# A two-block transformer kernel: squares, first norm, bias tables, memory rows and a token-major feed-forward, all changed at once

## The chip, the cores and the metric

The kernel runs on one core of a Trainium2 chip. The metric is the device time of one execution in microseconds (us). Three executions of the kernel before took 2737.11, 2744.5 and 2745.8 us; the median is 2744.5 us.

## The reference, cut to what matters

Everything is float32, the sequence has 256 tokens and the model 2048 features. The first block has two layers, the second one:

```
first block, for l in 0, 1:
    h = rms_norm(x, norm_g[l]);  z = h @ w_in[l]             # 2048 -> 16 heads, 4 x 128 columns each
    6 dilated heads (rotary), 6 neighbourhood heads (bias from na_rpb, + mask), 4 memory heads
    (the memory heads' keys and values: rms_norm(mem) @ w_mem_kv[l])
    x = x + (attention * silu(gate)) @ w_out[l]
second block:
    h = rms_norm(x);  z = h @ w_in;  state space mixer, differential attention with
    bias = rel_table[t5_bucket(k - q)], gates, x = x + m @ w_out
    h = rms_norm(x, norm2_w)
    x = x + (silu(h @ w_gate) * (h @ w_up)) @ w_down         # 2048 -> 5632 -> 2048
```

## The kernel before, in words

Activations are kept feature-major: `res`, `x_hi`, `x_lo` are [128 features, 16 blocks, 256 tokens]. A float32 product is made of three products of rounded parts: `w_hi*x_hi + w_hi*x_lo + w_lo*x_hi` (L1692 to L1694). Weights come in chunks of 512 KB, [128, 8*128], into a ring of four (`w_raw`, `RING`). SyncE loads chunk n+4 once `w_lo` of chunk n is made (L378), ScalarE rounds it to `w_hi` when TensorE has freed the slot (`split_hi`, L585), VectorE subtracts to `w_lo` (`split_lo`, L1077). A job is two chunks: 16 weight tiles, 48 matmuls of 256 token columns, for 128 output features. Four jobs are a period, one head takes one period, and there are 98 periods. Each engine's order is written out by hand; `prev` parts of a period work for the head before.

The names that matter for the change:

- Start. GpSimd squares `res` block by block and adds it up (L408, L403). TensorE sums the result over partitions with a matrix of ones (L1744, L1735) behind job 0 of the first period; VectorE makes `rstd` from it (`rstd_of`, L1098). The first weight chunk is split at block 3 of `x`.
- Neighbourhood bias. GpSimd stores the padded table of all 12 heads 64 times in `na_pad_d` in one transfer (L416), then for each of six heads loads four skewed pieces (L432), adds the mask (L436) and stores the bias (L438); then the second layer's six heads later.
- Memory. In heads 2 to 9 of layer 0 ScalarE rounds and squares two blocks of `mem` a head (`mem_blocks`, L621, L624); GpSimd adds the squares (L445), behind its six bias heads.
- Bias table of the second block. In the out projection of layer 0, behind jobs 4 to 11, TensorE makes one head's row of 511 values on all 128 partitions (L1767), VectorE copies it (L1287) and ScalarE's queue stores it in `rel_d` (L748). The same jobs make the state space tables: VectorE makes turns, ScalarE four activations (L601 to L606) and a store of 256 KB to `tab_d` (L608), whose landing it waits for before the next (`table`).
- Feed-forward. 11 groups of 4 feature blocks. In each: 4 gate jobs, 4 up jobs, 4 down jobs (`down`, L1978 to L1980), interleaved by `GATE_JOBS` and `UP_JOBS`. Gate and up are evacuated per 128 features (L1315), the sigmoid is ScalarE's (L946).

## Time and profile before

| | |
|---|---|
| median of three executions | 2744.5 us |
| the profiled execution | 2746.96 us |
| its span, first to last instruction | 2745.4 us |
| TensorE matmul busy | 2543.1 us, 93% |
| VectorE / ScalarE / GpSimd busy | 68% / 42% / 17% |
| first stretch, to 205.8 us: TensorE busy | 142.25 us |
| feed-forward, from about 1989 us to the end: TensorE busy | 749.15 of 756 us |

All times are microseconds from the span's start unless marked ns. PE is TensorE's matmul side, PEld its weight loads, DVE VectorE, ACT ScalarE, POOL GpSimd, SP SyncE; a q behind an engine's name is its sequencer or its transfer issues. "x" counts instructions. L12 is line 12. A transfer's landing time runs from issue to its last semaphore.

### The profile page before, as it was taken

Reading aid. Unit: us, or ns where it says so; the run is one execution under the profiler, and the core shown is the slowest. Engines: PE = TensorE matmul, PEld = TensorE weight load, DVE = VectorE, ACT = ScalarE, POOL = GpSimd, SP = SyncE. Lnnn points to the kernel's source line nnn. Section 1 sums busy time; section 2 is a strip of 40 time slices with the busy share of each in tenths; the row PEclk is TensorE's granted clock in tenths of the full one; section 3 lists DMA queues with packets and bytes.
Section 4 is the critical chain, followed back from the end, with each engine's and each line's share of the span. In section 5 each row is a group of like instructions: output and inputs, shape, how many; then the busy total and the mean of one; then the engine's idle time right before and its main releaser. Section 6 shows DMA issues by size and latency. Waiting matters only on the chain.

```text
span 2745.4 us, 54167 instructions
## 1 busy us (share of the span) xinstructions
PE 2543.1 (93%) x19776; PEld 2453.6 (89%) x19776; DVE 1877.5 (68%) x2716; ACT 1154.7 (42%) x1691; POOL 465.5 (17%) x501
## 2 busy tenths in 40 slices
PE   5779999989999999788888989699999999999999
PEld 5779999879999998778877777699999999999998
DVE  5667666778766667777778999665566555666654
ACT  3245444564444446544443222334433333333332
POOL 4310000123000002121136777310100000000000
PEclk8889999999999999999998999899999999999999
DMA  6655555567555555454444555465565555555554
GB/s 160 187 161 188 184 177 173 162 202 221 177 179 177 173 168 169 155 180 131 131 155 139 155 158 157 137 211 181 175 192 183 181 182 182 183 180 180 182 183 153
DMA packets 143166, 473.92 MB, mean 173 GB/s; under 512 B 18917, under 2 KB 25745, under 8 KB 142833
## 3 DMA queue, kind: packets, MB, share of 16 engines
q1 hardware_dynamic: 114048, 415.29, 47.1%
q0 software_dynamic: 9936, 28.44, 4.3%
q10 hardware_dynamic: 19104, 29.15, 3.2%
q8 instruction: 50, 0.82, 0.1%
q14 instruction: 28, 0.22, 0.0%
HBM read 447.01 MB, written 25.80 MB: 172 GB/s over the span
## 4 chain that ended last, share of the span: by engine, by line
PE 64%; DVE 14%; issue 10%; DMA 6%; ACT 3%; POOL 3%; DVEq 0%; ACTq 0%; POOLq 0%
PE z_ps L1692 17%; PE z_ps L1693 17%; PE z_ps L1694 17%; DVE w_lo L1077 5%; DMA tab_d<-arena 4%; DMA na_pad_d<-arena 1%; PE o_ps L1731 1%; PE s_ps L1713 1%; PE s_ps L1978 1%; PE s_ps L1979 1%; PE s_ps L1980 1%; PE o_ps L1980 1%; PE o_ps L1979 1%; PE o_ps L1978 1%; PE p_ps L1980 1%
## 5 line engine op out<-in xcount | busy, mean ns | idle before, releaser
L1077 DVE TENSOR_TENSOR w_lo<-w_raw,w_hi 128x1024 fp32r<-128x1024 f32 x782 | 985.3, 1291 | 434.5 <-ACT w_hi L585 422.8
L1692 PE MATMUL z_ps<-x_hi,w_hi 128*128 128x256 f32 x4224 | 1232.6, 292 | 49.9 <-DVE w_lo L1077 25.1
L1693 PE MATMUL z_ps<-x_lo,w_hi 128*128 128x256 f32 x4224 | 1212.5, 287 | 0.0
L1694 PE MATMUL z_ps<-x_hi,w_lo 128*128 128x256 f32 x4224 | 1210.9, 287 | 0.0
L585 ACT ACTIVATE w_hi<-w_raw 128x1024 fp32r<-128x1024 f32 x782 | 799.5, 1051 | 479.5 <-PE z_ps L1694 297.7
L1692 PEld LDWEIGHTS z_ps<-x_hi,w_hi 128*128 128x128 f32 x4224 | 829.1, 196 | 78.5 <-issue 64.2
L1693 PEld LDWEIGHTS z_ps<-x_lo,w_hi 128*128 128x128 f32 x4224 | 829.6, 196 | 1.4
L1694 PEld LDWEIGHTS z_ps<-x_hi,w_lo 128*128 128x128 f32 x4224 | 828.2, 196 | 0.0
L1692 PE MATMUL z_ps<-y_hi,w_hi 128*128 128x256 f32 x768 | 223.2, 291 | 25.3 <-DVE w_lo L1077 12.9
L1693 PE MATMUL z_ps<-y_lo,w_hi 128*128 128x256 f32 x768 | 220.6, 287 | 0.0
L1694 PE MATMUL z_ps<-y_hi,w_lo 128*128 128x256 f32 x768 | 220.3, 287 | 0.0
L1692 PEld LDWEIGHTS z_ps<-y_hi,w_hi 128*128 128x128 f32 x768 | 150.6, 196 | 35.3 <-issue 18.9
L1692 PE MATMUL z_ps<-m_hi,w_hi 128*128 128x256 f32 x576 | 167.7, 291 | 6.3 <-DVE m_lo L1512 3.6
L1694 PE MATMUL z_ps<-m_hi,w_lo 128*128 128x256 f32 x576 | 164.3, 285 | 0.0
L1693 PE MATMUL z_ps<-m_lo,w_hi 128*128 128x256 f32 x576 | 164.3, 285 | 0.0
L1693 PEld LDWEIGHTS z_ps<-y_lo,w_hi 128*128 128x128 f32 x768 | 150.8, 196 | 0.0
L1694 PEld LDWEIGHTS z_ps<-y_hi,w_lo 128*128 128x128 f32 x768 | 150.7, 196 | 0.0
L402 POOL TENSOR_TENSOR arena<-arena 128x256 f32<-128x256 f32 x32 | 26.5, 829 | 685.9 <-ACT arena L594 685.9
L1692 PEld LDWEIGHTS z_ps<-m_hi,w_hi 128*128 128x128 f32 x576 | 111.9, 194 | 7.8 <-DVE m_lo L1512 4.5
L1315 DVE TENSOR_TENSOR arena<-z_ps,rstd 128x256 f32<-128x256 f32 x120 | 50.7, 423 | 97.2 <-PE z_ps L1694 97.0
L1693 PEld LDWEIGHTS z_ps<-m_lo,w_hi 128*128 128x128 f32 x576 | 112.1, 195 | 0.4
L1694 PEld LDWEIGHTS z_ps<-m_hi,w_lo 128*128 128x128 f32 x576 | 111.8, 194 | 0.0
(314 smaller groups left out, 3202.4 us busy)
## 6 DMA issues: line engine op xcount, KB each, us to landing
w_raw<-in_w SPq DMA_DIRECT2D x784, 512.0 KB, 3.7
tab_d<-arena ACTq DMA_DIRECT2D x32, 256.0 KB, 5.0
res<-tab_d POOLq DMA_DIRECT2D x32, 256.0 KB, 2.9
sg_d<-arena ACTq DMA_DIRECT2D x32, 128.0 KB, 3.2
arena<-sg_d POOLq DMA_DIRECT2D x16, 256.0 KB, 3.9
arena<-in_dil_bias ACTq DMA_DIRECT2D x12, 256.0 KB, 2.8
arena<-na_pad_d POOLq DMA_DIRECT2D x48, 64.0 KB, 3.3
na_bias_d<-arena POOLq DMA_DIRECT2D x12, 256.0 KB, 2.9
```

Source lines behind the costliest of these rows:

```text
L402: pool.tensor_tensor(sq_sum[:, 1, :], sq_sum[:, 1, :], sqf[:], ALU.add)
L585: act.activation(w_hi[:, n % RING, :], w_raw[:, n % RING, :], ACT.Copy).then_inc(w_hi_ready, 1)
L1077: dve.tensor_tensor(w_lo[:, n % RING, :], w_raw[:, n % RING, :], w_hi[:, n % RING, :].bitcast(F32), ALU.subtract).then_inc(w_lo_ready, 1)
L1315: dve.tensor_tensor(dst, z_ps[c % ring][:, 0, :], rstd[:], ALU.mult).then_inc(z_free, 1)
L1692: pe.matmul(z, wh, hi[:, kt, :], start=(first and i == 0), stop=False)
L1693: pe.matmul(z, wh, lo[:, kt, :], start=False, stop=False)
L1694: m = pe.matmul(z, wl, hi[:, kt, :], start=False, stop=(last and i == len(kts) - 1))
L1713: m = pe.matmul(s_ps[:, t, :], q_t[:, t * P:(t + 1) * P], k_t[:], start=True, stop=True)
L1731: m = pe.matmul(o_ps[:, 0, :], v_tok[:, k, :], probs_t[:, k, :], start=(k == 0), stop=(k == NQ - 1))
L1978: pe.matmul(z, wh, y_hi[:, kt, :], start=(kt == 0), stop=False)
L1979: pe.matmul(z, wh, y_lo[:, kt, :], start=False, stop=False)
L1980: m = pe.matmul(z, wl, y_hi[:, kt, :], start=False, stop=(kt == F_GROUP - 1))
```

## The change

1. Squares of `x`: ScalarE squares four blocks in one activation of 128x1024 (4 of them); GpSimd adds them in 7 additions of 128x512. The first weight chunk is asked for behind the first quarter of `x` and is split at block 0.
2. The sums over partitions come behind job 1 instead of job 0 in both layers, and VectorE makes `rstd` behind the third pair of splits.
3. The padded neighbourhood table is stored once (`na_one_d`), and copied 64 times per head, DRAM to DRAM, in front of that head's four loads; GpSimd's loops over heads are unrolled.
4. The second block's bias table: one matmul for all 8 heads (8 partitions x 511), one copy, and 8 stores of ScalarE's queue that read one partition 64 times each, four behind job 7 and four behind job 11 of the out projection.
5. Memory blocks in heads 4 to 11; the state space constants one head later.
6. Feed-forward gate and up: tokens become the output's partitions. `x_hi`/`x_lo` tiles are the weights, four feature blocks of `w` the 512 moving columns. The result is scaled by `rstd` per partition (made on [128, 2] columns), the product [2, 128 tokens, 512] is turned back with 8 transposes a group. All 8 gate chunks, then 8 up chunks, then 8 down chunks. The down product is as before. The chunks are gathered from the same weight stream in runs of 256 floats, four per partition.

```diff
-            for n in range(KT):
-                pool.wait_ge(x_landed[n // 4], 16)
-                pool.wait_ge(sq_summed, summed(-1, n))
-                pool.tensor_tensor(sq[:], res[:, n, :], res[:, n, :], ALU.mult).then_inc(sq_ready, 1)
-                sum_squares(-1, n, False)
+            for i in range(4):
+                pool.wait_ge(sq_ready, 4 * i + 4)
...
+                    pool.tensor_tensor(sq_sum[:], sq_sum[:], lower, ALU.add).then_inc(xsq_step, 1)
...
-            pool.dma_start(na_pad_d.rearrange("c (h x) -> h c x", h=DEPTH * N_NA),
-                           rpb_pad.rearrange("h r x -> h (r x)").unsqueeze(1).to_broadcast(
-                               [DEPTH * N_NA, GRID_W, DR * DC])).then_inc(pad_stored, 16)
+            pool.dma_start(na_one_d, rpb_pad.rearrange("h r x -> h (r x)")).then_inc(pad_filled, 16)
...
+                    pool.dma_start(na_pad_d[lh:lh + 1].rearrange("h (c x) -> h c x", c=GRID_W),
+                                   na_one_d[lh:lh + 1].unsqueeze(1).to_broadcast([1, GRID_W, DR * DC])).then_inc(pad_stored, 16)
...
+                if n % 4 == 3:
...
+                    act.activation(x_sq[n // 4 % 2], res[:, n - 3:n + 1, :], ACT.Square).then_inc(sq_ready, 4)
...
-                with act.Fori(2, N_DIL) as h:
-                    head_period(p0 + h, l, h, ap["dil_bias"], mem=h - 2 if l == 0 else None)
+                with act.Fori(4 if l == 0 else 2, N_DIL) as h:
+                    head_period(p0 + h, l, h, ap["dil_bias"], mem=h - 4 if l == 0 else None)
...
-                        act.dma_start(rel_d[h].rearrange("(p x) -> p x", p=P),
-                                      rel_rows[:, h % 2, 0:REL]).then_inc(rel_stored[h % 2], 16)
+                        act.dma_start(rel_d[h:h + 1].rearrange("h (c x) -> h c x", c=CHUNK_ATT),
+                                      rel_rows[h:h + 1].unsqueeze(1).to_broadcast(
+                                          [1, CHUNK_ATT, REL])).then_inc(rel_stored, 16)
...
+            def ffn_gate(g):
+
+                dve.wait_ge(fg_s, g + 1)
+                for t in range(NQ):
+                    e = dve.scalar_tensor_tensor(out=act_t[:, t, :], in0=z_ps[t][:].rearrange("p a b -> p (a b)"),
+                                                 scalar=rstd_c[:, t:t + 1], in1=act_t[:, t, :],
+                                                 op0=ALU.mult, op1=ALU.mult)
...
+            def ffn_chunk(g, k, banks, wait_kt=False):
...
+                        pe.matmul(z[t], x_hi[:, kt, r], hi_w[:, :, i * P:(i + 1) * P], start=(kt == 0), stop=False)
+                        pe.matmul(z[t], x_lo[:, kt, r], hi_w[:, :, i * P:(i + 1) * P], start=False, stop=False)
+                pe.wait_ge(w_lo_ready, at + 1)
...
+                        m = pe.matmul(z[t], x_hi[:, kt, t * P:(t + 1) * P], lo_w[:, :, i * P:(i + 1) * P], start=False,
+                                      stop=(kt == KT - 1))
...
+            def turn_act(g, banks):
+
+                pe.wait_ge(fu_used, g + 1)
+                for h in range(2):
+                    for b in range(2):
+                        for t in range(NQ):
+                            m = pe.transpose(banks[h][:, b, t * P:(t + 1) * P],
+                                             act_t[:, t, (2 * h + b) * P:(2 * h + b + 1) * P], ident[:])
...
+            def blocks(base, j, step, n):
+
+                return bass.AP(ap["w"].tensor, (base + j // 4) * (P * CH * P) + (j % 4) * 2 * P,
+                               [[CH * P, P], [step * P * CH * P, n], [1, 2 * P]])
```

On TensorE in the first period, before (`p_ps<-arena,ones` are the sums over partitions; 48 matmuls are one job):

```order
L1694 MATMUL z_ps<-x_hi,w_lo 128x256
L1744 MATMUL p_ps<-arena,ones 128x256
L1735 MATMUL p_ps<-arena,ones 128x256
L1692 MATMUL z_ps<-x_hi,w_hi 128x256
L1693 MATMUL z_ps<-x_lo,w_hi 128x256
```

The pair is TensorE's instructions 49 and 50 there, behind 48 matmuls; in the changed kernel it is 97 and 98, behind 96, with the same neighbours.

On ScalarE in the out projection of layer 0, before, one job (`w_hi` is the split, the four activations in `arena` and `tab_d` the table, the next three the output block):

```order
L585 ACTIVATE w_hi<-w_raw 128x1024 x2
L601 ACTIVATE arena<-arena 128x256
L602 ACTIVATE arena<-arena 128x256
L604 ACTIVATE arena<-arena 128x256
L606 ACTIVATE arena<-arena 128x256
L608 DMA tab_d<-arena 128x512
L590 ACTIVATE x_hi<-res,gains 128x256
L593 ACTIVATE arena<-res,final_g 128x256
L594 ACTIVATE arena<-res 128x256
L748 DMA rel_d<-arena 128x511
```

And after, behind job 7 (and again behind job 11):

```order
L662 ACTIVATE x_hi<-res,gains 128x256
L665 ACTIVATE arena<-res,final_g 128x256
L666 ACTIVATE arena<-res 128x256
L826 DMA rel_d<-arena 64x1x511 x4
L657 ACTIVATE w_hi<-w_raw 128x1024 x2
L673 ACTIVATE arena<-arena 128x256
L674 ACTIVATE arena<-arena 128x256
L676 ACTIVATE arena<-arena 128x256
L678 ACTIVATE arena<-arena 128x256
L680 DMA tab_d<-arena 128x512
```

The eight single stores between jobs have become two runs of four, each ahead of the next table store on the same queue.

On TensorE in the feed-forward, before, three matmuls for one weight tile:

```order
L1692 MATMUL z_ps<-x_hi,w_hi 128x256
L1693 MATMUL z_ps<-x_lo,w_hi 128x256
L1694 MATMUL z_ps<-x_hi,w_lo 128x256
```

After, a part of a gate chunk of 12 (the next four of L2099 and L2100 repeat these), and the transposes:

```order
L2099 MATMUL z_ps<-w_hi,x_hi 128x512
L2100 MATMUL z_ps<-w_hi,x_lo 128x512
L2099 MATMUL z_ps<-w_hi,x_hi 128x512
L2100 MATMUL z_ps<-w_hi,x_lo 128x512
L2105 MATMUL z_ps<-w_lo,x_hi 128x512 x4
...
L2115 MATMUL p_ps<-ident,arena 128x128 x4
L2115 MATMUL o_ps<-ident,arena 128x128 x4
```

Twelve matmuls of 512 columns stand where 24 of 256 stood, and eight transposes a group are new.

## Rows read from the trace of the kernel before

**Rows 1.** Busy time by stretch: us, busy (count) per engine, TensorE's granted clock, DMA share, GB/s
```profile
0.00:205.80 205.80, 142.25 (x1018) 139.13 (x1019) 129.07 (x229) 70.61 (x110) 64.49 (x88) 0.85 0.61 169
205.80:480.20 274.40, 274.02 (x2221) 271.55 (x2220) 187.51 (x261) 132.49 (x200) 10.76 (x11) 1.00 0.56 181
2058.00:2606.00 548.00, 548.00 (x4569) 548.00 (x4568) 327.25 (x413) 216.93 (x256) 0.00 (x0) 1.00 0.57 182
```
**Rows 2.** TensorE to 156 us: start, us, instruction, idle before it and releaser
```profile
13.67 0.55 PE L1692 MATMUL z_ps<-x_hi,w_hi 128*128 128x256 f32 x1 [13.67 <-DVE w_lo L1070]
35.72 1.22 PE L1744 MATMUL p_ps<-arena,ones 128*128 128x256 f32 x2 [8.59 <-POOL arena L403]
75.53 0.55 PE L1692 MATMUL z_ps<-x_hi,w_hi 128*128 128x256 f32 x1 [12.28 <-DVE w_lo L1077]
152.49 2.07 PE L1731 MATMUL o_ps<-arena 128*128 128x256 f32 x4 [16.26 <-ACT arena L656]
```
**Rows 3.** VectorE in the first 32 us, same columns
```profile
8.10 2.86 DVE L1233 SCALAR_TENSOR_TENSOR x_lo<-res,gains,x_hi 128x256 fp32r<-128x256 f32 x4 [6.69 <-ACT x_hi L688]
24.75 6.52 DVE L1077 TENSOR_TENSOR w_lo<-w_raw,w_hi 128x1024 fp32r<-128x1024 f32 x4
```
**Rows 4.** ScalarE and GpSimd from 119 to 151 us, same columns
```profile
149.65 0.42 ACT L624 ACTIVATE arena<-arena 128x256 f32<-128x256 f32 x1 [26.80 <-POOL arena L445]
126.24 0.57 POOL L438 DMA_DIRECT2D na_bias_d<-arena  x1 [0.70 <-POOL arena L436]
146.15 0.57 POOL L438 DMA_DIRECT2D na_bias_d<-arena  x1 [0.70 <-POOL arena L436]
```
**Rows 5.** Transfers by line: issues, KB each, median us from issue to landing
```profile
tab_d<-arena ACTq DMA_DIRECT2D x32, 256.0 KB, 5.0
res<-tab_d POOLq DMA_DIRECT2D x32, 256.0 KB, 2.9
arena<-sg_d POOLq DMA_DIRECT2D x16, 256.0 KB, 3.9
na_pad_d<-arena POOLq DMA_DIRECT2D x1, 2667.0 KB, 39.3
rel_d<-arena ACTq DMA_DIRECT2D x8, 255.5 KB, 5.9
arena<-in_rpb POOLq DMA_DIRECT2D x1, 10.2 KB, 2.1
```
**Rows 6.** The same view, of 38 to 78 us
```profile
w_raw<-in_w SPq DMA_DIRECT2D x5, 512.0 KB, 25.1
```
**Rows 7.** TensorE at the start of layer 1, columns of rows 2
```profile
612.10 1.22 PE L1744 MATMUL p_ps<-arena,ones 128*128 128x256 f32 x2 [1.36 <-POOL arena L403]
618.88 0.55 PE L1692 MATMUL z_ps<-x_hi,w_hi 128*128 128x256 f32 x1 [4.71 <-DVE w_lo L1077]
```
**Rows 8.** Matmuls on y_hi, twelve jobs of each layer's out projection: us, busy, clock, DMA
```profile
518.40:601.10 82.70, 72.43 (x384) 0.98 0.66 214
1051.40:1133.30 81.90, 71.32 (x383) 1.00 0.62 189
```
**Rows 9.** Chain that ended last, 520 to 590 us: start, us, what
```profile
524.71 5.35 DMA tab_d<-arena
...
531.35 0.43 ACT arena L606
531.79 6.18 DMA tab_d<-arena
```
**Rows 10.** TensorE at 212 us, same columns as rows 2
```profile
211.99 0.38 PE L1711 MATMUL v_ps<-ident,arena 128*128 128x128 f32 x2
212.21 1.03 PE L1713 MATMUL s_ps<-arena 128*128 128x256 f32 x4
```
**Rows 11.** Line L1713: duration ns, min/median/max
```profile
L1713 PE MATMUL s_ps<-arena x128: 379/379/382, 62.2 to 1020.5; 128*128 128x256 f32 x128
```
**Rows 12.** Packets of 1800 to 1885 us, where sg_d is loaded in 1 KB runs
```profile
DMA packets 5249, 18.73 MB, mean 220 GB/s; under 512 B 680, under 2 KB 680, under 8 KB 5248
```

More of the change, by code:

```diff
@@ L974, in _ @@
+            with act.Fori(1, N_GROUPS - 1) as g:
+                ffn_group(g)
+            ffn_group(N_GROUPS - 1, last=True)
+            for q in range(3):
+                ffn_split(N_GROUPS, q + 1)
         @block.vector
```

479 lines of the change are left out of this document (300 added, 179 removed).

## The prediction

> **What bounds the kernel now.** I read the busy shares, then the busy time by stretch, then TensorE's idle times with their releasers, then the chain and the transfers. The kernel is bound by TensorE almost everywhere, but for three kinds of places. In the feed-forward TensorE is busy 548.00 of 548.00 us at full clock, 4569 matmuls, one every 119.9 ns [rows 1]; nothing else can shorten that stretch. From 205.8 to 480.2 us it is the same (274.02 of 274.40). In the first 205.8 us it is busy 142.25 [rows 1], and four waits make up 50.8 of the 63.6 us of idle time: 13.67 for the first weights, 8.59 for GpSimd's sum of squares, 12.28 for weights, 16.26 for ScalarE, which stands 26.80 us behind GpSimd's addition of memory squares [rows 2, 4]. In the out projections a job is not TensorE's alone: the chain runs through the store of a table, 5.35 and 6.18 us, and the activations behind it [rows 9].
>
> **Start.** (a) Squares. GpSimd's 32 operations become 7, and the sum is asked for one job later. VectorE works without a pause from 8.10 us through the four splits that start at 24.75 [rows 3], and that work stays, so job 0 ends about where it did (35.72 - 8.59 = 27.1 us) though it begins some 3 us earlier. What goes is the wait of 8.59. What is late next is job 1's weights, made at 24.75 to 31.3, so no more than a microsecond of it comes back. (b) Table. The transfer of 2667 KB took 39.3 us [rows 5], and weight chunks issued beside it took 25.1 us to land [rows 6]. The 12.28 us stall is this. The new copies are 222 KB each; a twelfth of the old bytes, 3.3 us at the old rate, behind a landing of at least 2.1 [rows 5]. I take 5 us with the issue for each; no weight chunk waits long beside that, so 12.28 goes. (c) Memory. GpSimd's bias heads came every (146.15 - 126.24) / 2 = 10.0 us [rows 4]; now 15. They start some 12 us of squares and 39 of table earlier, at about 35 us, and six end at about 125. ScalarE wants GpSimd's first addition in head 4. The second period starts at 27.1 + 3 x 5.8 = 44 us, a period of 206 matmuls takes 206 x 274.4 / 2221 = 25.5 [rows 1], and the addition stands three jobs into the fifth: 44 + 3 x 25.5 + 17 = 138 us. TensorE bears 26.80 - 16.26 = 10.5 more. So 16.26 goes too, unless a copy costs over 5 + (138 + 10.5 - 125) / 6 = 8.9 us. Sum: 8.6 + 12.3 + 16.3 = 37.2, less 1: **-36 us**. Bounds: -20 if the memory wait stays, -46 if the small waits between go as well, and the constants that move a head later cost nothing.
>
> **Layer 1's norm.** The sums behind job 1 leave the waits of 1.36 and 4.71 [rows 7] without a reason: the splits of job 3 now come ahead of VectorE's wait. Next late is the split of the next head's first chunk, some 11 us behind the sums against two jobs of 11.5. **-6 us**; bounds 0 and -9.
>
> **Bias table of the second block.** Removed are 7 matmuls, 7 copies and 7 stores. I count nothing for them: the twelve jobs with and beside them took 82.70 us in layer 0 and the same twelve without them 81.90 in layer 1 [rows 8], because the table store binds when they do not. So 0.8 goes at most. Added are 8 stores of 64 x 2 KB = 128 KB, each read from one partition, four in a row ahead of the next table store, on its queue (the order above; such a store is on the chain [rows 9]). ScalarE waits for that store to land before the table after it, and its next splits stand behind this wait. The price of such a store isn't in the trace. From both sides: the old table, read from 12 partitions, moved 2667 / 39.3 = 67.9 KB/us [rows 5]. If one partition can give all of that, a store is 1.9 us; if it gives a twelfth, 5.65 KB/us, 22.6 us. I take 5.6, near the geometric middle and near the other bias store of 5.9 [rows 5]. Then four are 22.4 us. The table store is issued 5.2 us behind the first (4 issues, two splits, four activations), so it lands 17.2 later than alone, and the issues cost 1.4: 18.6 a batch, 37 for two, less 0.8: **+36 us**. Bounds: 1.9 us gives (7.6 - 5.2 + 1.4) x 2 - 0.8 = +7; 22.6 us gives (90.4 - 5.2 + 1.4) x 2 - 0.8 = +172.
>
> The Trainium skill, "SBUF — State Buffer", Door 1 (the port swizzle), says that four neighbouring partitions share one of 16 transfer ports. By it the old table's 12 partitions reached three ports, so one gave 22.6 KB/us, and a partition read 64 times would give that too: 5.7 us a store. It agrees with the value taken and speaks against this part of the change; no row of before shows one port alone.
>
> **Feed-forward.** Gate and up were 88 jobs of 48 matmuls, 4224 x 119.9 ns = 506.5 us. They become 11 x 16 x 12 = 2112 matmuls of 512 columns. No rounded matmul of that width is in the trace. From both sides: if time follows columns, 239.8 ns, no gain; if 256 columns are held up by something that doesn't grow, such as the weight load (PEld is as busy as PE, 548.00 us [rows 1]), 512 take what 213 ns of streaming take. The nearest row is a plain float32 pass of 256 columns, with a 128x128 load for each: four passes in 1.03 us, the last 0.379 long, so (1.03 - 0.379) / 3 = 217 ns from one to the next [rows 10, 11], twice 107 ns of streaming at 2.4 GHz and nearly nothing more. I take 217: 458.3 us, -48.2. Added are 88 transposes at 110 ns (two from 211.99 to 212.21 [rows 10]), 9.7. The evacuations are about the same on VectorE and ScalarE, which are busy 327 and 217 of 548 us [rows 1], and the ring keeps three chunks (7.8 us) between a freed slot and its use. **-38 us**; bounds -41 and +12.
>
> **Sum.** 2747.0 (the profiled execution; 1.6 us around its span) - 36 - 6 + 36 - 38 = 2703. That execution is 2.5 us above the median of the runs, so I predict **2700 us**.
>
> **Rivals.** All times are against the runs' median.
> - *Cheap stores.* One partition gives the whole 67.9 KB/us: 2700 - 29 = 2671. For it: nothing in the trace shows a single partition to be slow. Against it: 12 partitions got only 67.9 while weights reach over 200 GB/s [rows 12].
> - *No gain by width.* Matmul time follows columns: 2700 + 48 = 2748, no change. For it: TensorE's and the loads' busy time are equal and tell nothing apart. Against it: the 217 ns pass.
> - *Slow stores: slower than before.* One partition gives 5.65 KB/us; table stores stand 90 us behind each four, twice: 2700 + 136 = 2836. The point from which this decides is a store of about 11 us: then each four is 44, a batch 40 and both cost 80, which is all that the rest brings. For it: 25.1 us landings beside the old table [rows 6].
> - *Starved chunks: slower.* The gathers in 1 KB runs become the bound of gate and up. For it: loads of sg_d in such runs landed in 3.9 us against 2.9 for res in 2 KB runs, 256 KB both [rows 5]; two such a chunk make 2 us more. With two chunks in flight one would come every 3.0 us against 12 x 217 ns = 2.6 wanted: 176 x 0.4 = 70, 2770. Against it: 220 GB/s moved with such loads in flight [rows 12], and 512 KB in 2.6 us is 201. It decides from 2.6 us a chunk.
>  [...] The four runs of a chunk lie 2 MiB apart. [...]
> - *Memory wait stays.* Copies of 12 us or more: 2716.
>
> **Chances.** Forecast 0.50 (2685 to 2715), cheap stores 0.26, no gain by width 0.06, slow stores 0.09, starved chunks 0.05, memory wait 0.04. A measurement of this kernel tells 0.3%, 8 us, from no change. Faster takes the forecast, cheap stores and the memory wait, 0.80; same the third, 0.06; slower the two others, 0.14. The range, 2652 to 2755, takes in cheap stores with the best of the other bounds and no gain by width, and leaves out slow stores and starved chunks.
>
> **What would show it.** Start: no wait over 3 us behind the sum, none on weights at 60 to 80 us, none on memory squares; the sum's matmuls at 33 to 36 us, the 206 us of before reached some 36 earlier. Norm: the two waits at layer 1 gone. Bias: the landing of `rel_d` stores (5.6 each, some 20 for the last of four), table stores landing over 15 us twice, TensorE idle beside them. Feed-forward: matmuls 217 ns apart, 2112 of them, TensorE busy throughout, PEld well under PE. I am wrong in sign if `rel_d` stores take over 11 us each or if `w_hi` waits for `w_raw` in the feed-forward.

## The result, and the profile after

The changed kernel takes **2694.8 us** (median, 2691.8 to 2696.8), the kernel before beside it 2744.3: a ratio of 0.982 with a 95% interval of 0.981 to 0.984, 49.5 us less. The profiled execution's span is 2695.2 us.

I cut both traces at the same points of the program: each mark is the moment at which ScalarE starts to split the first weight chunk of a stage, rounded to 0.1 us.

| stage, us | before | after | difference | predicted |
|---|---|---|---|---|
| start, to layer 0's out projection | 476.9 | 426.5 | -50.4 | -36 |
| layer 0's out projection | 121.2 | 144.4 | +23.2 | +36 |
| layer 1's start (two heads) | 56.3 | 55.6 | -0.7 | -6 |
| from there to the feed-forward | 1315.4 | 1316.4 | +1.0 | 0 |
| feed-forward, to the end of the span | 775.6 | 752.3 | -23.3 | -38 |

The busy time by stretch, the same view and stretches as [rows 1]; columns: us, busy (count) of TensorE, its weight loads, VectorE, ScalarE, GpSimd, granted clock, DMA share, GB/s:

```profile
0.00:205.80 205.80, 183.52 (x1430) 181.04 (x1431) 162.55 (x279) 97.49 (x147) 51.51 (x68) 0.97 0.64 209
...
2058.00:2606.00 548.00, 548.00 (x3183) 486.22 (x3182) 309.01 (x309) 223.76 (x228) 0.00 (x0) 1.00 0.69 186
```

In the first 205.8 us TensorE is idle for 22.3 us, where it was 63.6, and its granted clock is 0.97, where it was 0.85. The second number is a gain of its own that the prediction didn't count. In the feed-forward TensorE is busy throughout, as before, with fewer and wider matmuls; the loads no longer fill the stretch (486 of 548 us).

**Start.** What TensorE waited for up to 160 us, in total, times, longest (left out: 0.8 us for w_lo):

```profile
PE z_ps L1828 <- DVE w_lo L1166: 15.2, 2, 10.4
PE p_ps L1858 <- DVE arena L1246: 6.3, 2, 3.9
```

Against [rows 2]: the waits for the sum (8.59), for weights beside the big table (12.28) and for ScalarE's memory squares (16.26) are all gone, and the first matmul comes at 10.38 us (13.67 before). What stays are small waits that before had too: 4.82 for the second weight chunk (3.47 before), 3.86 and 2.39 for VectorE ahead of `p_ps` (3.63 and 4.74). GpSimd, whose bias heads come 17.4 us apart, ends the sixth in time:

```profile
134.98 0.58 POOL L508 DMA_DIRECT2D na_bias_d<-arena  x1 [0.30 <-POOL arena L506]
144.81 1.13 POOL L515 TENSOR_TENSOR arena<-arena 128x256 f32<-128x256 f32 x1 [9.26 <-ACT arena L696]
```

The second row is the first memory addition. It is GpSimd that waits here, 9.26 us, for ScalarE; in [rows 4] ScalarE waited 26.80 us for GpSimd.

**Bias table.** ScalarE and its queue in layer 0's out projection, start, us, instruction (ACTq is the issue of a transfer by ScalarE), idle before it:

```profile
495.59 0.62 ACTq L826 DMA_DIRECT2D rel_d<-arena  x1
...
496.92 13.88 ACTq L826 DMA_DIRECT2D rel_d<-arena  x2
510.90 2.00 ACT L657 ACTIVATE w_hi<-w_raw 128x1024 fp32r<-128x1024 f32 x2 [14.16 <-issue]
```

The first two of four stores are issued in 0.6 us each. The third and fourth take 13.88 us to issue: the engine itself is held, not a wait in its code, and behind it stand the splits that TensorE needs. The second batch does the same for 7.20 us, and the table store behind it lands after 12.0. The transfers from 496 to 515 us (queue, packets, MB, share of the 16 engines' time; then issues, KB each, median landing):

```profile
q10 hardware_dynamic: 423, 0.74, 77.6%
...
w_raw<-in_w SPq DMA_DIRECT2D x2, 512.0 KB, 6.5
rel_d<-arena ACTq DMA_DIRECT2D x4, 127.8 KB, 16.4
tab_d<-arena ACTq DMA_DIRECT2D x1, 256.0 KB, 6.5
```

ScalarE's queue takes 77.6% of the time of all 16 transfer engines and moves 0.74 MB in 19 us with it, 39 KB/us. Some of these bytes are table stores. Where the bias stores have the transfer engines to themselves, the last two numbers are the busy share and GB/s:

```profile
505.50:514.00 8.50, 0.73 (x3) 0.73 (x4) 2.01 (x2) 3.03 (x5) 0.00 (x0) 0.50 0.86 27
```

So 86% of 16 engines' time moves 27 KB/us. The four stores, issued from 495.59 us on, have landed by 518.77, 23.2 us later, and the second batch takes 21.9. TensorE pays with its idle time and then with its clock:

```profile
513.27 0.58 PE L1828 MATMUL z_ps<-y_hi,w_hi 128*128 128x256 f32 x1 [13.19 <-DVE w_lo L1173]
513.65 0.41 PE L1829 MATMUL z_ps<-y_lo,w_hi 128*128 128x256 f32 x1
513.87 0.41 PE L1830 MATMUL z_ps<-y_hi,w_lo 128*128 128x256 f32 x1
...
519.24 0.28 PE L1829 MATMUL z_ps<-y_lo,w_hi 128*128 128x256 f32 x1
519.36 0.28 PE L1830 MATMUL z_ps<-y_hi,w_lo 128*128 128x256 f32 x1
```

The stretch of the slow ones, in the view of busy times (the granted clock is the third number from the end):

```profile
513.30:518.50 5.20, 5.20 (x24) 5.20 (x25) 3.24 (x6) 3.71 (x8) 1.29 (x2) 0.50 0.87 141
```

Behind the 13.19 us of idle time the same matmul comes every 213 ns, and from 519 us on every 120. The granted clock of the stretch is 0.50, so 1.2 GHz, and 2.4 after it: 24 matmuls lose 93 ns each, 2.2 us. Over the whole first stage, rounded matmuls whose next one starts 195 to 230 ns later number 137 before and 72 after; against 119.9 ns they lose 12.7 and 6.6 us.

**Layer 1's start.** Against [rows 7]:

```profile
583.12 0.39 PE L1828 MATMUL z_ps<-x_hi,w_hi 128*128 128x256 f32 x1 [1.06 <-DVE x_lo L1261]
590.79 0.55 PE L1828 MATMUL z_ps<-x_hi,w_hi 128*128 128x256 f32 x1 [7.04 <-DVE w_lo L1173]
```

The wait for the sum is gone, and the wait for the low halves has grown from 4.71 to 7.04 us. (The 1.06 us for `x_lo` were 2.47 before.)

**Feed-forward.** Four matmuls of 512 columns that stand together, one before them, and four of the 88 transposes (0.60 us):

```profile
2199.76 0.60 PE L2115 MATMUL p_ps<-ident,arena 128*128 128x128 f32 x4
...
2202.26 0.39 PE L2100 MATMUL z_ps<-w_hi,x_lo 128*128 128x512 f32 x1
2202.48 1.07 PE L2105 MATMUL z_ps<-w_lo,x_hi 128*128 128x512 f32 x4
```

(1.07 - 0.39) / 3 = 227 ns from one to the next, where 217 were predicted. The gathered chunks don't starve it; landings in this stretch:

```profile
w_raw<-in_w SPq DMA_DIRECT2D x129, 512.0 KB, 5.0
w_raw<-in_w SPq DMA_DIRECT2D x66, 384.0 KB, 4.9
w_raw<-in_w SPq DMA_DIRECT2D x66, 128.0 KB, 2.9
```

### The profile page after: what moved, and what is told of

The parts are those of the page before. It is cut to its first block, busy times and chain, and to the rows that moved or that the text cites. A ratio compares the mean times of both kernels' runs of the same rounds, so it can differ in the third digit from the quotient of the medians.

```text
span 2695.2 us, 49472 instructions
## 1 busy us (share of the span) xinstructions
PE 2511.3 (93%) x17740; PEld 2345.2 (87%) x17740; DVE 1834.5 (68%) x2555; ACT 1164.6 (43%) x1652; POOL 455.7 (17%) x487
## 4 chain that ended last, share of the span: by engine, by line
PE 64%; DVE 16%; issue 10%; DMA 4%; ACT 3%; ACTq 1%; POOL 1%; DVEq 0%; POOLq 0%
PE z_ps L1828 11%; PE z_ps L1829 11%; PE z_ps L1830 11%; PE z_ps L2099 6%; PE z_ps L2100 6%; PE z_ps L2105 6%; DVE w_lo L1173 5%; DMA tab_d<-arena 4%; ACT w_hi L657 1%; PE o_ps L1867 1%; PE s_ps L1849 1%; ACTq L826 1%; PE o_ps L2134 1%; PE o_ps L2133 1%; PE o_ps L2132 1%
## 5 line engine op out<-in xcount | busy, mean ns | idle before, releaser
L1828 PE MATMUL z_ps<-x_hi,w_hi 128*128 128x256 f32 x2816 | 830.6, 295 | 34.9 <-DVE w_lo L1166 15.2
L1829 PE MATMUL z_ps<-x_lo,w_hi 128*128 128x256 f32 x2816 | 810.8, 288 | 0.0
L1830 PE MATMUL z_ps<-x_hi,w_lo 128*128 128x256 f32 x2816 | 809.7, 288 | 0.0
L1828 PEld LDWEIGHTS z_ps<-x_hi,w_hi 128*128 128x128 f32 x2816 | 555.2, 197 | 62.5 <-issue 50.2
L1829 PEld LDWEIGHTS z_ps<-x_lo,w_hi 128*128 128x128 f32 x2816 | 555.6, 197 | 1.3
L1830 PEld LDWEIGHTS z_ps<-x_hi,w_lo 128*128 128x128 f32 x2816 | 554.5, 197 | 0.0
L2099 PE MATMUL z_ps<-w_hi,x_hi 128*128 128x512 f32 x704 | 275.1, 391 | 0.6 <-DVE res L1694 0.6
L2100 PE MATMUL z_ps<-w_hi,x_lo 128*128 128x512 f32 x704 | 274.2, 389 | 0.0
L2105 PE MATMUL z_ps<-w_lo,x_hi 128*128 128x512 f32 x704 | 188.2, 389 | 0.0
L2099 PEld LDWEIGHTS z_ps<-w_hi,x_hi 128*128 128x128 f32 x704 | 132.2, 188 | 27.7 <-DVE res L1694 0.8
```

The lines of the kernel that those rows point to most:

```text
L1828: pe.matmul(z, wh, hi[:, kt, :], start=(first and i == 0), stop=False)
L1829: pe.matmul(z, wh, lo[:, kt, :], start=False, stop=False)
L1830: m = pe.matmul(z, wl, hi[:, kt, :], start=False, stop=(last and i == len(kts) - 1))
L2099: pe.matmul(z[t], x_hi[:, kt, r], hi_w[:, :, i * P:(i + 1) * P], start=(kt == 0), stop=False)
L2100: pe.matmul(z[t], x_lo[:, kt, r], hi_w[:, :, i * P:(i + 1) * P], start=False, stop=False)
L2105: m = pe.matmul(z[t], x_hi[:, kt, t * P:(t + 1) * P], lo_w[:, :, i * P:(i + 1) * P], start=False, stop=(kt == KT - 1))
```

## The experiments

Each kernel is the changed one with one edit, but for mem_old, which moves two things, and combined, which brings several edits together. Times are medians, with their range; `before` beside them took 2741 to 2747 us. The stages were cut as above:

| kernel | us (range) | ratio to before (95%) | start | out proj. 0 | layer 1 start | feed-forward |
|---|---|---|---|---|---|---|
| changed | 2694.8 (2691.8-2696.8) | 0.982 (0.981-0.984) | 426.5 | 144.4 | 55.6 | 752.3 |
| ffn_old | 2713.7 (2712.6-2715.7) | 0.988 (0.985-0.991) | 425.0 | 142.8 | 56.1 | 775.5 |
| rel_old | 2664.9 (2660.9-2671.1) | 0.971 (0.968-0.974) | 425.3 | 116.2 | 56.3 | 752.3 |
| rel_16 | 2668.9 (2662.4-2678.1) | 0.972 (0.969-0.976) | 425.5 | 116.0 | 58.3 | 752.3 |
| rel_spaced | 2663.2 (2661.8-2668.9) | 0.970 (0.967-0.973) | 424.2 | 118.3 | 56.1 | 752.2 |
| norm_old | 2686.3 (2685.1-2690.0) | 0.978 (0.976-0.981) | 425.8 | 142.8 | 54.8 | 752.2 |
| tab_wait | 2693.7 (2691.4-2697.4) | 0.981 (0.978-0.984) | 425.7 | 141.2 | 56.8 | 752.3 |
| tab_two | 2677.2 (2675.1-2678.3) | 0.975 (0.972-0.978) | 425.1 | 133.1 | 55.8 | 752.3 |
| pad_old | 2718.3 (2716.9-2719.2) | 0.991 (0.989-0.993) | 449.8 | 143.5 | 58.0 | 752.3 |
| mem_old | 2718.4 (2714.9-2724.6) | 0.991 (0.989-0.994) | 452.5 | 143.1 | 56.8 | 752.2 |
| first_old | 2690.7 (2689.3-2699.3) | 0.982 (0.979-0.984) | 427.2 | 140.0 | 55.4 | 752.3 |
| combined | 2638.8 (2634.9-2640.8) | 0.961 (0.959-0.963) | 424.2 | 107.4 | 51.2 | 752.3 |

The part from 176 chunks on to the feed-forward, in which no edit but tab_two's and combined's changes an instruction, takes 1310 to 1316 us in these single profiles. Differences of 5 us between kernels are therefore not read as effects unless a stage shows them. The out projections scatter too: where no edit touches them, layer 0's takes 140.0 to 144.4 us and layer 1's 115.3 to 120.3. The changed kernel's profile is at the upper end of all three.

### The feed-forward

**ffn_old** takes the feed-forward and its weight stream back:

```diff
-            for k in range(16):
-                ffn_chunk(0, k, z_ps[0:2] if k < 8 else z_ps[2:4], wait_kt=k < 8)
...
+            for k in range(8):
+                job2(P_FFN + k // 4, k % 4, x_hi, x_lo,
+                     (lambda kt: pe.wait_ge(x_lo_ready, (DEPTH + 1) * KT + kt + 1)) if k == 0 else None)
...
```

> The changed kernel with the feed-forward, and the weight stream that feeds it, as before the change (88 jobs of 48 matmuls of 256 columns). Theory: what is left of the time by this part is what the two traces show between the first split of the feed-forward and the end, 775.6 against 752.3 us, so this kernel takes 2694.8 + 23.3 = 2718 us (2714 to 2722), with matmuls 119.9 ns apart. Rival: the stretch is shorter only because the waits at its start and end (1.92 and 2.46 us of before) are gone and the rest is a shift between the stages; then it takes 2694.8 + 4.4 = 2699.

Measured 2713.7, 18.9 us over the changed kernel; its feed-forward takes 775.5 us, before's time to 0.1 us, so this part is worth 23.2 us as a stage. The rival is out; the expected 2718 is 4 us too high. (In the whole time some 4 us of it are hidden by the scatter of the other stages.)

**probe** adds matmuls behind the last one, when the other engines have nothing left to do:

```diff
+            def probe(n, stat, mov, cols):
+                for i in range(n):
+                    pe.matmul(zw[i % 4][:, 0:cols], stat(i), mov[i % len(mov)][:, 0:cols], start=True, stop=True)
...
+            probe(32, blk, wide, 512)
+            probe(32, one, wide, 512)
+            probe(32, blk, wide, 384)
...
+            probe(8, lambda i: ident[:], plain, 256)
```

> The changed kernel with matmuls added behind its last one, nothing else on the chip at work: rounded ones of 512, 384, 256, 128 and 64 columns with a new stationary block each, of 512 and 256 with the same one, and plain float32 ones of 512, 256 and 128. Theory: a rounded matmul takes its columns at 2.4 GHz plus a fixed 13 ns, whatever its width: 227, 173, 120 ns, and then, at 128 (53 + 13 = 66) and 64, it may meet the time of the weight load; with the same block the same, 227 and 120. Rival: the 120 ns at 256 columns are the time of the weight load, as the prediction's value of 217 ns at 512 assumed; then 384 columns take 160 and 512 take 213 to 217, and 128 and 64 columns take 120. The added matmuls lengthen the kernel by some 35 to 50 us.

One run, 2745.1 us, 50 us over the changed kernel. TensorE's matmuls by stretch (us, busy and count, granted clock): 512, 384, 256, 128 and 64 columns rounded, then plain 512 and 256. A count includes one or two under way at the edges. The first plain ones are left out: from 2728.8 to 2733.2 us the granted clock is 0.61, and four of them start 853 ns apart.

```profile
2694.30:2708.40 14.10, 14.10 (x64) 1.00 0.09 37
2709.30:2714.00 4.70, 4.70 (x29) 1.00 0.00 0
2714.80:2721.70 6.90, 6.90 (x60) 1.00 0.00 0
2721.95:2725.20 3.25, 3.25 (x32) 1.00 0.00 0
2725.40:2728.70 3.30, 3.30 (x33) 1.00 0.00 0
2733.20:2737.40 4.20, 4.20 (x11) 1.00 0.00 0
2737.50:2740.85 3.35, 3.35 (x17) 1.00 0.00 0
```

The starts of the matmuls are 226.7, 173.3, 119.9, 111 to 112 and 112 ns apart; with the same stationary block 226.7 and 119.9 again, though that block is loaded for every matmul too (32 loads for 32 matmuls). Columns at 2.4 GHz are 213.3, 160.0 and 106.7 ns, so a rounded matmul of 256 to 512 columns costs 13.3 ns beside them, and at 128 and 64 columns something that isn't shown holds it at 112. Plain float32 matmuls show two records each, 429.3 and 215.9 ns apart, two passes a record: 214.6 and 107.9 ns a pass, 1.3 over the columns. The loads are not what holds the 256-column matmuls, since the narrower ones, with a load each, come every 112 ns; and the plain pass was the wrong row to size a rounded one by. The clock did something unforeseen here: it fell to 0.50 at 2729 us, though TensorE had had no idle time, behind 3.4 us of 64-column matmuls back to back; the run doesn't show why.

### The bias table

**rel_old** takes the table back: eight matmuls, eight stores from 128 partitions, one a job.

```diff
-                    pe.matmul(rel_ps, rel_lhs[:, :, 0], one_hot, start=True, stop=True).then_inc(rel_mm, 1)
+                        if l == 0 and 0 <= 4 * i + c - REL_AT < N_DH:
+                            rel_row(4 * i + c - REL_AT)
...
-                        for c in range(4):
-                            rel_store(4 * (i - 1) + c)
+                        if l == 0:
+                            rel_store(4 * i + c)
```

> The changed kernel with the second block's bias table as before: eight matmuls, and eight stores from 128 partitions, one in each job. Theory: the table is all of the 23.2 us by which layer 0's out projection grew (121.2 to 144.4), so 2694.8 - 23.2 = 2671.6 us (2667 to 2676), no wait of TensorE over 3 us from 490 to 580 us. Rival: most of the growth is ScalarE's and VectorE's new order and one-off, the old stores cost as much as the new; then 2690 or more.

**rel_16** keeps one matmul and the four stores in a row, and changes where they read:

```diff
-                    pe.matmul(rel_ps, rel_lhs[:, :, 0], one_hot, start=True, stop=True).then_inc(rel_mm, 1)
+                    pe.matmul(rel_ps, rel_lhs.rearrange("p a (b c) -> p (a b) c", c=8)[:, :, 0], one_hot, start=True, stop=True).then_inc(rel_mm, 1)
...
-                        act.dma_start(rel_d[h:h + 1].rearrange("h (c x) -> h c x", c=CHUNK_ATT),
-                                      rel_rows[h:h + 1].unsqueeze(1).to_broadcast(
-                                          [1, CHUNK_ATT, REL])).then_inc(rel_stored, 16)
+                        act.dma_start(rel_d[h].rearrange("(p c x) -> p c x", p=16, c=4),
+                                      rel_rows[16 * h:16 * h + 16].unsqueeze(1).to_broadcast(
+                                          [16, 4, REL])).then_inc(rel_stored, 16)
```

> The changed kernel, but the one matmul makes each head's row on 16 partitions, and each of the eight stores reads these 16, four times each, instead of one 64 times. Bytes, packet size (2044), number, place and order of the stores are the same. Theory: a store from one partition is slow because all its packets come out of one narrow way; 16 partitions give several times the rate, a store lands within 3 to 4 us instead of 15, ScalarE isn't held at the issue, and the time falls by some 20 us to 2675 (2670 to 2680). Rival: the stores are slow by their packets or by four standing in a row on one queue; then nothing changes: 2695, holds of 14 and 7 us at the issue.

**rel_spaced** keeps the reads from one partition and spreads the stores:

```diff
-                        out_rest(i)
                         for c in range(4):
+                            split_hi(po + i, c + 1)
+                            table(KT * l + 4 * i + c - 2)
+                            out_block(po + i, c - 1, l, 4 * i + c - 1)
                             rel_store(4 * (i - 1) + c)
```

> The changed kernel with the same eight stores from one partition, issued one in each job (of about 6.9 us) instead of four in a row. Theory: what costs is the backlog of four (ScalarE held at the issue of the third and fourth, 13.88 and 7.20 us, and a table store behind them); a single store of some 5.6 us is nearly through when the next table store comes, which then lands 1 to 3 us late: 2694.8 - 15 = 2680 us (2673 to 2688). Rival: each store's own time goes onto the path wherever it stands: eight times 3 us or more, 2695 or above.

All three give 2663 to 2669, each below the range expected for it, and out projections of 116.0 to 118.3 us: 26 to 28 us back. rel_16, with one matmul and one copy, and rel_old, with eight of each, take the same time in the stage, so taking seven of each away gains nothing. The landing of the stores and the load that ScalarE's queue puts on the transfer engines, 425 to 570 us, in rel_16, then in rel_spaced:

```profile
q10 hardware_dynamic: 3184, 5.70, 10.9%
...
rel_d<-arena ACTq DMA_DIRECT2D x8, 127.8 KB, 5.2
```
```profile
q10 hardware_dynamic: 3184, 5.70, 20.9%
...
rel_d<-arena ACTq DMA_DIRECT2D x8, 127.8 KB, 6.7
```

The same packets and bytes cost half as much of the transfer engines' time from 16 partitions a head. But one partition alone is not dear enough to matter either: a single store lands in 6.7 us, within a job. It takes both, one source and four in a row; each remedy by itself takes all of the cost away. In rel_16 the issue of the third and fourth store is short:

```profile
492.76 1.47 ACTq L826 DMA_DIRECT2D rel_d<-arena  x2
```

I had expected rel_spaced at 2680, with each table store late by 1 to 3 us; it is 17 us better than that. The theories of rel_16 and rel_spaced are not rivals; they are two factors of one backlog. That reading from few partitions is slow in itself agrees with what the prediction took from the Trainium skill ("SBUF — State Buffer", Door 1): by it 4 stores of 5.7 us are 23, and the two batches needed 23.2 and 21.9. (That the two remedies are each enough is shown; a store from one partition on another engine's queue was not tried.)

### Layer 1's start

**norm_old** puts layer 1's norm back behind job 0:

```diff
+                if norm and l == 1:
+                    pe.wait_ge(sq_summed, summed(l, 0) - 1)
+                    pe.matmul(p_ps[:, 0, :], ones[:], sq_sum[:, 0, :], start=True, stop=True)
+                    column_sums(p_ps[:, 1, :], sq_sum[:, 1, :], sums_ready)
...
                 job(p, 1, m_hi if mem else x_hi, m_lo if mem else x_lo)
-                if norm:
+                if norm and l == 0:
```

> The changed kernel with layer 1's norm (sums on TensorE, root, reciprocal) behind job 0 as before; layer 0's stays one job later. Theory: the wait at layer 1's start (7.04 us in the changed kernel, 1.36 and 4.71 before) belongs to the last table store, for which VectorE waits before it makes the first low halves of layer 1, and not to the norm; moving the norm back costs 0 to 1 us: 2695 us (2692 to 2698), and TensorE's idle time at 585 to 600 us stays within 1 us of the changed kernel's. Rival (the prediction's step): the norm's place is worth 6 us: 2701, with the wait on VectorE's rstd back.

**tab_wait** moves a wait of VectorE:

```diff
-                dve.wait_ge(tab_stored, 16 * KT * (l + 1))
+                if l == DEPTH - 1:
+                    dve.wait_ge(tab_stored, 16 * KT * (l + 1))
...
                     split_lo(p, 3)
+                    if l > 0:
+                        dve.wait_ge(tab_stored, 16 * KT * l)
                     dve.wait_ge(sums_ready, l + 1)
```

> The changed kernel with one wait moved: VectorE waits for layer 0's last table store not at the end of the out projection but behind layer 1's first three splits, ahead of the first write into the table's buffer. Theory: the 7.04 us of TensorE's idle time at layer 1's start are that wait, so most of it goes, until ScalarE's halves (behind the last table's activations) are late next: 3 to 5 us less, 2691 us. Rival: ScalarE's splits of layer 1 are as late as VectorE's, nothing changes: 2695. By the prediction's step nothing is left to win here once the norm is moved: 2695 as well.

TensorE at layer 1's start in norm_old, then in tab_wait:

```profile
580.81 0.39 PE L1831 MATMUL z_ps<-x_hi,w_hi 128*128 128x256 f32 x1 [0.73 <-DVE x_lo L1263]
582.78 0.70 PE L1883 MATMUL p_ps<-arena,ones 128*128 128x256 f32 x2 [1.35 <-POOL arena L465]
588.48 0.55 PE L1831 MATMUL z_ps<-x_hi,w_hi 128*128 128x256 f32 x1 [4.57 <-DVE w_lo L1175]
```
```profile
586.69 0.55 PE L1831 MATMUL z_ps<-x_hi,w_hi 128*128 128x256 f32 x1 [6.97 <-DVE w_lo L1173]
```

With the norm early, 0.73 + 1.35 + 4.57 = 6.7 us are idle and the sum's matmuls fall into the gap; with the norm late, 1.06 + 7.04 = 8.1. The low halves of the next chunk are late at the same moment either way, so the prediction's step is refuted. My reason for it, VectorE's wait for the table store, falls too: with that wait gone the 6.97 us stay. In the changed kernel the two ended together: the store lets VectorE start at 589.41 us, and ScalarE's first half, begun at 588.26, is ready after its 1.06 us, at 589.32; to take away one of them alone wins nothing. What is late is one step further up; VectorE and ScalarE in tab_wait:

```profile
585.32 4.63 DVE L1173 TENSOR_TENSOR w_lo<-w_raw,w_hi 128x1024 fp32r<-128x1024 f32 x4 [3.69 <-ACT w_hi L657]
```
```profile
581.66 0.42 ACT L673 ACTIVATE arena<-arena 128x256 f32<-128x256 f32 x1 [2.43 <-DVE arena L1280]
...
584.23 3.90 ACT L657 ACTIVATE w_hi<-w_raw 128x1024 fp32r<-128x1024 f32 x4 [0.95 <-ACT arena L678]
```

ScalarE waits 2.43 us for the turns of the last table, makes it, and only then splits layer 1's chunks. combined, below, supports this: there ScalarE splits two of these chunks ahead of the last table, the wait is 3.20 us instead of 7.04, and the stage takes 51.2 us; but combined changes more than that. In the whole time norm_old is 8.5 us below the changed kernel, with ranges that don't overlap. The stage accounts for 0.8 of that, layer 0's out projection for 1.6; the rest lies in stages whose instructions are the same, and I leave its cause open.

### The start

**pad_old** writes the neighbourhood table in one go again, **mem_old** puts the memory blocks back into heads 2 to 9 and with them the state space constants one head earlier (both are point 5 of the change), **first_old** loads all of x ahead of the first chunk and splits that chunk behind the fourth block:

```diff
-                    pool.dma_start(na_pad_d[lh:lh + 1].rearrange("h (c x) -> h c x", c=GRID_W),
-                                   na_one_d[lh:lh + 1].unsqueeze(1).to_broadcast([1, GRID_W, DR * DC])).then_inc(pad_stored, 16)
...
+            pool.dma_start(na_pad_d.rearrange("h (c x) -> h c x", c=GRID_W),
+                           rpb_pad.rearrange("h r x -> h (r x)").unsqueeze(1).to_broadcast(
+                               [DEPTH * N_NA, GRID_W, DR * DC])).then_inc(pad_stored, 16)
```
```diff
-                with act.Fori(4 if l == 0 else 2, N_DIL) as h:
-                    head_period(p0 + h, l, h, ap["dil_bias"], mem=h - 4 if l == 0 else None)
+                with act.Fori(2, N_DIL) as h:
+                    head_period(p0 + h, l, h, ap["dil_bias"], mem=h - 2 if l == 0 else None)
...
-                head_period(p0, l, 0, "dil", norm=True, prev=False, prev2=False)
-                head_period(p0 + 1, l, 1, "dil", prev2=False, extra=(step_sizes, turn_counts) if l == 0 else None)
+                head_period(p0, l, 0, "dil", norm=True, prev=False, prev2=False,
+                            extra=(step_sizes, turn_counts) if l == 0 else None)
```
```diff
-            load_x(0)
-            sp.dma_start(w_raw[:, 0, :], ap["w"][0]).then_inc(w_landed[0], 16)
-            for i in range(1, 4):
+            for i in range(4):
                 load_x(i)
-            for r in range(1, RING):
+            for r in range(RING):
...
-                if n == 0:
+                if n == 3:
                     split_chunk_hi(0)
```

> The changed kernel with the table of the neighbourhood heads written as before in one go (12 rows, 64 times each, 2667 KB, read from 12 partitions of the arena), ahead of the mask. Theory: while its some 39 us last (27 to 67 us), chunks of the weight stream land late and TensorE waits some 12 us, as before; GpSimd's six bias heads (11 to 12 us each without the copies) end at about 74 + 6 x 11.5 = 143 us, just ahead of the memory addition that ScalarE wants at 144.8 us, so that wait stays away: 2694.8 + 12 = 2707 us, and 2 to 4 more by a lower granted clock, 2710. Rival: the memory blocks two heads later give the weights no cover, but the first weights, taken earlier, do: nothing, 2695. Other rival: both waits come back, 2694.8 + 28 = 2723.

> The changed kernel with the memory blocks in heads 2 to 9 as before. Theory: ScalarE wants GpSimd's first addition some two heads (51 us) earlier, at about 94 us, while GpSimd ends its sixth bias head at about 136 us (copies of 4.3 us included); ScalarE stands 42 us, TensorE bears 10.5 of it, and 30 us of TensorE's idle time come back, more than the 16.26 of before: 2694.8 + 30 = 2725 us (2718 to 2735). Rival: the copies a head at a time are what took the wait away, and the move of the memory blocks only keeps it away: 2695 to 2700.

> The changed kernel with x loaded whole ahead of the first chunk of weights, and that chunk split behind the fourth block of x, as before. Theory: TensorE's first matmul, at 7.5 us in the changed kernel and 13.67 in before, comes 5 to 6 us later, and nothing of this is made up: 2694.8 + 6 = 2701 us. Rival (the prediction counted 1 us for it): the splits of x set the pace of job 0 on VectorE wherever it begins, and job 0 ends where it did: 2695 to 2696.

**pad_old** costs 23.5 us, 23.3 of them in the first stage, twice the stall I had priced. Transfers from 25 to 80 us, and TensorE's waits for weights to 160 us:

```profile
w_raw<-in_w SPq DMA_DIRECT2D x12, 512.0 KB, 10.2
na_pad_d<-arena POOLq DMA_DIRECT2D x1, 2667.0 KB, 40.1
```
```profile
PE z_ps L1827 <- DVE w_lo L1172: 17.3, 5, 6.6
```

Not one wait of 12.28 but five that make 17.3, and 117 slow matmuls against 72 in the stage (4.2 us). The memory wait stayed away, as expected.

**mem_old** costs 23.6 us, 26.0 in the first stage. ScalarE stands 26.96 us behind the first memory addition, and TensorE 18.6:

```profile
124.80 0.42 ACT L696 ACTIVATE arena<-arena 128x256 f32<-128x256 f32 x1 [26.96 <-POOL arena L515]
```
```profile
PE o_ps L1872 <- ACT arena L728: 18.6, 1, 18.6
```

I had expected 30, with GpSimd's sixth bias head at 136 us; it issues that head's store at 121.4 us here and at 135.0 in the changed kernel (why its heads are faster here isn't shown). The memory wait is not all of the cost: TensorE also waits 5.03 us for weights at 49 us, where 16 small operations of VectorE for the constants stand ahead of the split, and 2.73 at 87 us. The changed kernel has neither wait, so the later place of the constants is worth something too. The two runs divide the work: the copies by heads do not take the memory wait away, the move of two heads does, even beside the big transfer (pad_old); and what the copies take away are the waits for weights.

**first_old** shows 2690.7, no slower than the changed kernel. Its first matmul is at 13.31 us (10.38 in the changed kernel, where I had written 7.5), its chunk 8 is split 1.8 us later, and 0.7 us of it are left at the end of the stage. The rival holds: the earlier first weights are worth nothing, as the prediction had counted.

### What binds the out projections, and a faster kernel

**tab_two** gives the rotation table two buffers:

```diff
-        tab_out = part(1, 2, pair)
+        tab_out = [part(1, 2, pair)]
+        top[0] = heads_at + 14
+        tab_out.append(part(1, 2, pair))
...
-                    act.wait_ge(tab_stored, 16 * st)
+                    act.wait_ge(tab_stored[par], 8 * (st - par))
```

> The changed kernel with two buffers for the rotation table that ScalarE makes in the out projections, so that ScalarE no longer waits for a table's store to land before it makes the next. Theory: the store of the table is what binds both out projections: layer 1's takes 120 us for 16 jobs whose 768 matmuls at 119.9 ns need 92; with two buffers ScalarE's own 5.4 us a job are under TensorE's 5.76, and layer 1's falls to 95 to 100 us, layer 0's by 10 to 20, since of a batch of four bias stores the holds at the issue stay: 2694.8 - 22 - 15 = 2658 us (2645 to 2670). Rival: the chain through VectorE's and ScalarE's table operations binds by itself and the landing lies beside it: less than 5 us, 2690 or more.

2677.2: better by 17.6 us, half of what I expected. Layer 0's out projection falls by 11.3 us. Layer 1's takes 115.7 instead of 120.3, and there the landing was said to be all; but that lies within the 115.3 to 120.3 of kernels whose layer 1 is untouched, so nothing is shown to be won there. The scatter is that of the landings: ScalarE waits 15.8 us in all for them in the changed kernel's layer 1 and 1.8 in rel_spaced's, with the same instructions. What binds when the landings are quick is the round between VectorE and ScalarE, here VectorE, then ScalarE:

```profile
1018.10 0.49 DVE L1265 SCALAR_TENSOR_TENSOR x_lo<-res,gains,x_hi  x1 [0.93 <-ACT x_hi L665]
```
```profile
1017.41 0.51 ACT L665 ACTIVATE x_hi<-res,gains  x1 [1.11 <-DVE res L1263]
...
1021.24 0.42 ACT L677 ACTIVATE arena<-arena 128x256 f32<-128x256 f32 x1 [0.71 <-DVE arena L1284]
```

ScalarE waits for VectorE's sum, VectorE for ScalarE's upper half, ScalarE for VectorE's turns: 6.6 to 6.9 us a job, against TensorE's 5.76.

**combined** brings the repairs together: one store of all bias rows, read from 128 partitions four times each (1022 KB), the two table buffers, the moved wait of tab_wait, and these two changes of order, on VectorE and on ScalarE:

```diff
                         split_lo(po + i, c + 1)
-                        out_block(po + i, c - 1, l, 4 * i + c - 1)
+                        out_add(po + i, c - 1, 4 * i + c - 1)
                         table(KT * l + 4 * i + c - 1)
+                        out_lower(l, 4 * i + c - 1)
...
                 out_block(po + KT // 4 - 1, 3, l, KT - 1)
-                table(KT * l + KT - 1)
+                if l == 0:
+                    split_hi(PERIODS_LAYER, 1)
+                table(KT * l + KT - 1, 1)
```

> The changed kernel with the repairs the runs so far point to: the bias rows on 128 partitions and written by one store (each partition four times); two buffers for the rotation table; VectorE makes the next table's turns ahead of the low half of x, for which it waits on ScalarE; ScalarE splits layer 1's first two chunks ahead of layer 0's last table; the wait for that table's store stands ahead of the first write over it. Theory: the stores of the bias rows cost 30 us (as in the runs without them), the round between VectorE and ScalarE in the out projections (6.6 to 6.9 us a job against TensorE's 5.76) some 15 to 20 us each, layer 1's start 5: 2694.8 - 30 - 38 - 5 = 2622 us (2610 to 2645). Rival: with the stores repaired the out projections are bound by what they were before the change (about 117 us each): 2660.

**2638.8 us**, a ratio of 0.961 (0.959 to 0.963): 56 us below the changed kernel and 102 below before. The out projections of both layers, us, busy, clock:

```profile
424.00:532.00 108.00, 103.56 (x842) 101.62 (x841) 90.76 (x146) 72.62 (x138) 20.24 (x27) 1.00 0.66 200
938.00:1046.00 108.00, 103.56 (x842) 102.56 (x840) 91.57 (x147) 71.75 (x137) 19.55 (x26) 0.98 0.59 188
```

TensorE is now busy 96% of both, and they take 107.4 and 107.3 us (121.2 and 120.9 before). Layer 1's start takes 51.2 us, 4.4 less. The out projections stay 9 us above the 98 or so that follow from the expectation (117 less 19), and the whole is 17 us above 2622. What the single repairs share of this was not taken apart.

## Why the prediction was right or wrong

The forecast, 2700 us, is 5 us off, and the likeliest case did come. That the total fits so well is luck: three of the four terms were 13 to 15 us off, start and table came out 27.2 us better, feed-forward and norm 20.0 worse, and the errors cancel.

- **Start, -36 predicted, -50.4 measured.** The three waits that were named are the ones that went. The step that was mis-sized is the price of the weights beside the big table, 12.28: one wait was read as the whole effect, while the transfer also makes smaller waits and a slower clock behind them; by pad_old it is worth 23.3. The memory term, 16.3, was too small as well: mem_old loses 26.0 in the stage, 18.6 by the memory wait and 5.0 where the constants stand, whose move was counted at nothing. The prediction had no term for the clock (6.1 us of the 50.4). That the memory wait goes, and that the earlier first weights win nothing, held (mem_old, first_old). The squares themselves and the sum's later place were not undone alone. The three runs already make 50.0 together (23.3, 26.0, 0.7), so the effects overlap, and what the squares are worth by themselves is open.
- **Layer 1's norm, -6 predicted, 0 measured (norm_old).** The step "the splits of job 3 now come ahead of VectorE's wait" was true and beside the point: the 4.71 us of [rows 7] were for w_lo, and I took its releaser to be the norm ahead of it in the code. ScalarE was late with the chunk, behind the last table.
- **Bias table, +36 predicted, +23.2 measured; 28 to 30 by rel_old.** Right in kind: four stores from one partition, 23.2 and 21.9 us for four (22.4 predicted), stand in a row and hold up ScalarE. The store's own price, 5.6, was good. The step that failed is the path: not the landing of the table store behind them, which was to come 17.2 us late and took 6.5 and 12.0 from its issue. What holds ScalarE was not foreseen: its issue of the third and fourth is itself held for 13.88 and 7.20 us. That taking the old eight rows away gains nothing agrees with rel_16 against rel_old.
- **Feed-forward, -38 predicted, -23.3 measured.** 2112 matmuls at 226.7 instead of 217 ns are 20.5 us more. 506.5 - 478.8 = 27.7, less 9.7 for the transposes, is -18.0, and the waits at the two ends, 4.4 us before, are 0.6, with 15 slow matmuls behind the last of them that the changed kernel doesn't have (1.4 us): -23.1 in all. The better bound, -41, doesn't follow from its own terms either; 2112 x 213.3 ns and the transposes give -46. The step that failed is the row: a plain float32 pass has next to no fixed cost, and a rounded matmul has 13.3 ns.
- **Rivals.** Cheap stores are out: the stores cost 23 to 30 us, and the kernel comes near that rival's 2671 only in rel_16 and rel_spaced, which repair them. No gain by width (2748) is out, since half of the cost beyond the columns did go. Starved chunks are out: from 2058 to 2606 us ScalarE waits 3.9 us in all for w_raw, VectorE not at all, and TensorE is never idle. The Trainium skill ("DMA: Bandwidth & Descriptors", Latency and other measured facts) has 164 GB/s for copies in which the rows of neighbouring partitions lie 2 MiB apart. Here it is the four runs of one partition that lie so; the stretch moves 186 GB/s without a wait, and no run shows a limit of that kind. The memory wait stayed only where the memory blocks were left early.

## What to carry to other kernels

Size a new operation by a row of the same kind of operand, not by the nearest width: what a rounded matmul costs beyond its columns was the same at 256, 384 and 512, so wider ones pay it less often. A transfer's price is its rate times how many stand in a row: spread small stores that read few partitions over the work, or let them read many partitions, and look twice at the queue of an engine that feeds TensorE (another engine's queue was not tried here). A wait is put down to what ended it last; before moving anything, ask of that releaser what it waited for itself, up to two engines back. Terms that are each some 14 us off can still add up to a good total; compare them stage by stage.

## What the runs showed of the hardware

- A rounded float32 matmul takes its columns at 2.4 GHz plus 13.3 ns (226.7, 173.3 and 119.9 ns for 512, 384 and 256 columns), with a new or the same stationary block, a load for each, and about 112 ns at 128 columns and at 64. A plain float32 pass takes 1.3 ns beyond its columns at 512 and 256.
- An engine that issues a transfer can be held at the issue: 11.41 us for one store of 128 KB behind three others from one partition. The chain of waits of the changed kernel (start, us, what):

```profile
499.40 11.41 ACTq L826
```

- 16 transfer engines can be 86% busy at 27 KB/us when the bytes are read 64 times from one partition. Of the same packets and bytes, read from 16 partitions a head, they spend half the time (10.9% against 20.9%).
- Behind 13 us of idle time TensorE ran 24 matmuls at 1.2 GHz before it was back at 2.4, which adds 2.2 us to the wait; over the start this made 12.7 us before and 6.6 after.
- The granted clock can fall without idle time: it was 0.50 at 2729 us of probe, behind 32 matmuls of 64 columns back to back, and four plain matmul records came 853 ns apart instead of 429.
